# Query and key of the second mixer: one product of 512 columns in place of two of 256, and banks shared anew

## The reference

```python
def mlstm_mixer(h, w_in, b_i, b_f, g_head, w_out):
    proj = (h @ w_in).astype(jnp.float32)
    q, k, v, o, i_raw, f_raw = jnp.split(
        proj, np.cumsum([ML_QK_WIDTH, ML_QK_WIDTH, ML_V_WIDTH, ML_V_WIDTH, ML_HEADS]).tolist(), axis=-1)
    ...
    _, hs = lax.scan(_mlstm_chunk_step, init, (qc, kc, vc, ic, fc))
    ...
    out = (jax.nn.sigmoid(o) * hs).astype(h.dtype)
    return out @ w_out
```

## Time and profile before

| | |
|---|---|
| median of three runs | 1743.56 us |
| lowest, highest | 1743.27, 1744.08 us |
| the profiled execution | 1744.14 us, its span 1742.4 us |
| TensorE busy | 90% of the span |
| VectorE busy | 42% |
| ScalarE busy | 24% |
| mixer of layer 1: first group | 875.24 to 955.98 us |
| its groups 1, 2, 3 | from 955.98, 1027.38, 1098.78 to 1170.19 us |
| its output stage | 1170.19 to about 1276 us |

### The profile page before, as it was taken

The page is one execution under the profiler, slowest core; times in us unless marked ns, Lnnn a source line. Parts: engine busy times, 40 slices in busy tenths (PEclk is TensorE's granted clock), DMA queues, the critical chain, the costliest instruction groups (busy, mean ns, idle before and its releaser), DMA issues.

```text
span 1742.4 us, 25494 instructions
## 1 busy us (share of the span) xinstructions
PE 1572.3 (90%) x9954; PEld 1080.8 (62%) x9954; DVE 731.9 (42%) x1170; ACT 424.3 (24%) x572; POOL 44.4 (3%) x70
## 2 busy tenths in 40 slices
PE   8999999999997789778899999999999887688776
PEld 8999999888544244324397988988864343234322
DVE  5544444443342233222364857657434332233213
ACT  6344343433000000000154333333320000000002
POOL 0010000100100000000011000000000000000000
PEclk9999999999998998889799999999999998898888
DMA  7645455578999999999954465575799999999996
GB/s 259 212 153 177 153 169 182 209 288 308 381 423 423 426 426 424 425 427 425 412 180 159 154 195 172 165 265 206 252 368 424 426 424 424 427 426 424 425 426 243
DMA packets 160785, 543.88 MB, mean 312 GB/s; under 512 B 17504, under 2 KB 34064, under 8 KB 127824
## 3 DMA queue, kind: packets, MB, share of 16 engines
q1 hardware_dynamic: 151232, 541.12, 79.8%
q10 hardware_dynamic: 9040, 0.49, 0.3%
q0 software_dynamic: 448, 1.36, 0.2%
HBM read 540.83 MB, written 2.10 MB: 312 GB/s over the span
## 4 chain that ended last, share of the span: by engine, by line
PE 68%; DMA 21%; SPq 5%; DVE 2%; issue 1%; ACT 1%; DVEq 0%; ACTq 0%
PE psum_G L755 35%; DMA ring<-in_moe_w 21%; PE psum_S L755 18%; PE psum_A L755 9%; SPq L556 5%; PE psum_T L755 5%; DVE w_lo L434 1%; ACT w_hi L430 1%; PE psum_A L762 0%; DMA x<-in_x 0%; ACT arena L1308 0%; DVE x L1855 0%; DVE h L2108 0%; PE psum_T L1009 0%; PE psum_T L762 0%
## 5 line engine op out<-in xcount | busy, mean ns | idle before, releaser
L755 PE MATMUL psum_A<-ring,arena 128*32 128x512 f32 x1984 | 289.4, 713 | 133.5 <-DMA ring<-in_moe_w 130.8
L434 DVE TENSOR_TENSOR w_lo<-ring,w_hi 128x2048 fp32r<-128x2048 f32 x126 | 289.1, 2298 | 280.5 <-ACT w_hi L430 278.3
L430 ACT CAST w_hi<-ring 128x2048 fp32r<-128x2048 f32 x127 | 241.9, 1906 | 238.5 <-PE psum_G L755 152.2
L755 PEld LDWEIGHTS psum_A<-ring,arena 128*32 128x32 f32 x1984 | 67.2, 120 | 301.6 <-issue 300.4
L1988 DVE COPY arena_two<-psum_A 128x512 f32<-128x512 f32 x64 | 44.3, 692 | 365.7 <-PE psum_T L755 336.3
L2020 DVE TENSOR_TENSOR x<-x,psum_S 128x512 f32<-128x512 f32 x128 | 88.0, 688 | 166.8 <-PE psum_S L755 166.8
L755 PE MATMUL psum_G<-xT_hi,w_hi 128*128 128x256 f32 x512 | 149.5, 292 | 0.0
L755 PE MATMUL psum_G<-xT_hi,w_lo 128*128 128x256 f32 x512 | 145.0, 283 | 0.0
L755 PE MATMUL psum_G<-xT_lo,w_hi 128*128 128x256 f32 x512 | 145.0, 283 | 0.0
L1517 ACT ACTIVATE arena<-psum_T 128x64 f32<-128x64 f32 x64 | 14.4, 224 | 473.4 <-PE psum_T L755 473.4
L755 PE MATMUL psum_G<-arena,h 128*128 128x128 f32 x1024 | 126.8, 284 | 0.0
(11 more groups left out here) (244 smaller groups left out, 2150.6 us busy)
## 6 DMA issues: line engine op xcount, KB each, us to landing
ring<-in_moe_w SPq DMA_DIRECT2D x368, 1024.0 KB, 19.1
ring<-in_ml_w_in SPq DMA_DIRECT2D x48, 1024.0 KB, 5.1
ring<-in_sb_w_in SPq DMA_DIRECT2D x47, 1024.0 KB, 5.1
ring<-in_sb_w_out SPq DMA_DIRECT2D x16, 1024.0 KB, 5.0
turned_slots<-in_moe_w SPq DMA_DIRECT2D x16, 1024.0 KB, 13.2
ring<-in_ml_w_out SPq DMA_DIRECT2D x16, 1024.0 KB, 5.1
x<-in_x SPq DMA_DIRECT2D x4, 512.0 KB, 8.2
out_x<-h SPq DMA_DIRECT2D x4, 512.0 KB, 2.7
```

Of the source, the lines that this page charges most:

```text
L430: act.copy(w_hi[:, slot_place(j), :], ring[:, slot_place(j), :]).then_inc(hi_made, 1)
L434: dve.tensor_tensor(w_lo[:, slot_place(j), :], ring[:, slot_place(j), :], w_hi[:, slot_place(j), :].bitcast(F32), ALU.subtract).then_inc(l ...
L755: return pe.matmul(dst, lhsT, rhs, start=start, stop=stop, skip_group_check=True)
```

## The change

Query and key no longer share a bank. Query goes into `G{hd}` (slots 0, 1), key into `S{hd}` (slots 2, 3). For each block, one product moves `xT_pair[:, :, k, :]`, the high and the low part of the turned x side by side (2 x 256 columns), past the high part of the weights into the whole bank; a second one moves the high part past the low weights into the first half. The two halves of the bank must then be added when they are taken out: VectorE copies the second half into `qkT` and adds the first. For the query this is a step of its own at position 17 (`take_query`); the key is taken at the old place, and then both are multiplied with the row of scales. The head scores wait for `query_key_ready` instead of the emptied banks. Values move from S to G and the gate from G to S in layer 1; layer 0 stays as it is.

```diff
+QUERY_STEPS = [(17, "query", 0)]
...
-    SCHEDULES[_layer, "group"] = schedule(_steps, 14, GROUP_ENDS)
+    SCHEDULES[_layer, "group"] = schedule(_steps + (QUERY_STEPS if _layer else []), 14, GROUP_ENDS)
...
-        xT_hi = sb("xT_hi", [P, KT, T], F32R)
-        xT_lo = sb("xT_lo", [P, KT, T], F32R)
+        xT_pair = sb("xT_pair", [P, 2, KT, T], F32R)
+        xT_hi, xT_lo = xT_pair[:, 0], xT_pair[:, 1]
...
-        def group_bank(c, b):
-            return f"{'GSG'[c]}{b}"
+        def group_bank(layer, c, b):
+            return f"{('GSG', 'SGS')[layer][c]}{b}"
...
-                            begin(hd)
+                            bank = f"{'GS'[j // 2]}{hd}"
+                            if j % 2 == 0:
+                                claim(bank, chunk_use(1, i, 0, hd) if j else query_use(i, hd))
...
-                                last = three_turned(psum[f"G{hd}"][:, (j // 2) * T:(j // 2 + 1) * T], k,
-                                                    (slot_place(j), slice(kk * FF + hd * P, kk * FF + (hd + 1) * P)),
-                                                    k == 0, k == KT - 1)
-                                if k == KT - 1 and j == 3:
-                                    last.then_inc(filled[f"G{hd}"], 1)
+                                part = slice(kk * FF + hd * P, kk * FF + (hd + 1) * P)
+                                mm(psum[bank][:, :].rearrange("p (n t) -> p n t", n=2), w_hi[:, slot_place(j), part],
+                                   xT_pair[:, :, k, :], k == 0, False)
+                                last = mm(psum[bank][:, 0:T], w_lo[:, slot_place(j), part], xT_hi[:, k, :], False, k == KT - 1)
+                                if k == KT - 1:
+                                    last.then_inc(filled[bank], 1)
...
                     if k == 0:
-                        wait_chunk(1, g, 0)
+                        pe.wait_ge(query_key_ready, g * MLG + MLG)
...
+                elif layer and c == 0:
+                    sum_halves(1, [chunk_filled(1, i, 0, n) for n in range(MLG)], "S")
+                    for n in range(MLG):
+                        dve.tensor_tensor(qkT[:, n, :, :], qkT[:, n, :, :], rstd_row.unsqueeze(1).to_broadcast([P, 2, T]), ALU.mult)
+                    dve.drain().then_inc(query_key_ready, MLG)
...
+            def sum_halves(m, ready, banks):
+
+                for n in range(MLG):
+                    dve.wait_ge(*ready[n])
+                    dve.tensor_copy(qkT[:, n, m, :], psum[f"{banks}{n}"][:, T:2 * T])
+                dve.drain()
+                for n in range(MLG):
+                    bank = f"{banks}{n}"
+                    dve.tensor_tensor(qkT[:, n, m, :], qkT[:, n, m, :], psum[bank][:, 0:T], ALU.add).then_inc(emptied[bank], 1)
+                dve.drain()
+
+            def take_query(i):
+
+                sum_halves(0, [(filled[f"G{n}"], query_use(i, n) + 1) for n in range(MLG)], "G")
```

More of the change, by code:

```diff
@@ L114 @@
 for _layer, _steps in ((0, SB_STEPS), (1, ML_STEPS)):
-    SCHEDULES[_layer, "first"] = (schedule(GATE_STEPS, 14, GROUP_ENDS) if _layer else
+    SCHEDULES[_layer, "first"] = (schedule(GATE_STEPS + QUERY_STEPS, 14, GROUP_ENDS) if _layer else
                                   schedule(FIRST_X_STEPS, 14, FIRST_X_ENDS, split_from=3))
-    SCHEDULES[_layer, "group"] = schedule(_steps, 14, GROUP_ENDS)
+    SCHEDULES[_layer, "group"] = schedule(_steps + (QUERY_STEPS if _layer else []), 14, GROUP_ENDS)
     SCHEDULES[_layer, "out"] = schedule(_steps, 16, OUT_ENDS, 0.75, ROUTER_STEPS)
@@ L138, in bank_uses @@
             phase(("gates", layer), T=1, A=ML_HEADS // 2)
[L139 removed]
+        phase(("mix", layer), G=2 * NGROUP, S=(2 if layer else 1) * NGROUP, T=(3 if layer else 2) * NGROUP, A=(1 if layer else 2) * NGROUP)
         phase(("out", layer), G=2, S=2)
@@ L372, in turned_bank, with chunk_use, query_use @@
             return order[u], first_use["norm_mix", layer][order[u]] + order[:u].count(order[u])
-        def group_bank(c, b):
-            return f"{'GSG'[c]}{b}"
+        def group_bank(layer, c, b):
+            return f"{('GSG', 'SGS')[layer][c]}{b}"
+        def chunk_use(layer, i, c, b):
+            if layer:
+                return i * 2 + (first_use["mix", 1][group_bank(1, c, b)] + (c > 0))
+            return i * (1 if c == 1 else 2) + (first_use["mix", 0][group_bank(0, c, b)] + c // 2)
         def chunk_filled(layer, i, c, b):
-            bank = group_bank(c, b)
-            return filled[bank], i * (1 if c == 1 else 2) + (first_use["mix", layer][bank] + c // 2 + 1)
+            return filled[group_bank(layer, c, b)], chunk_use(layer, i, c, b) + 1
+        def query_use(i, hd):
+            return i * 2 + first_use["mix", 1][f"G{hd}"]
         def out_filled(layer, c, b):
@@ L392, in value_parts @@
             c = value_chunk(layer)
-            bank = group_bank(c, b)
+            bank = group_bank(layer, c, b)
             if layer:
@@ L415, in split_was_read @@
                 done = sum(1 for _, m in OUT_ORDER[:j + 1] if m < 3)
-                return split_read, layer * (9 * NGROUP + 12) + 9 * NGROUP + done
+                return split_read, layer * (9 * NGROUP + 12) + (8 if layer else 9) * NGROUP + done
             c = j // 4
@@ L419, in split_was_read @@
                 return chunk_filled(layer, i, c, 1)
+            if layer and j == 1:
+                return filled["G1"], query_use(i, 1) + 1
+            if layer:
+                return split_read, i * 8 + (9 * NGROUP + 12 + 3 * c + j % 4 + 1 - (j > 1))
             return split_read, i * 9 + (layer * (9 * NGROUP + 12) + 3 * c + j % 4 + 1)
@@ L890, in begin @@
                         if j % CSLOT == 0:
-                            bank = group_bank(c, n)
-                            claim(bank, i * (1 if c == 1 else 2) + (base[bank] + c // 2))
+                            claim(group_bank(layer, c, n), chunk_use(layer, i, c, n))
                     if layer == 0 and isinstance(i, int) and i == 0 and j == 0:
@@ L932, in project @@
                                 event(8 * j + 4 * (hd // 2) + kk)
-                            bank = group_bank(c, hd // 2)
+                            bank = group_bank(0, c, hd // 2)
                             last = three_turned(psum[bank][:, (hd % 2) * T:(hd % 2 + 1) * T], k,
@@ L944, in project @@
                                 event(8 * j + 4 * b + kk)
-                                last = three(psum[group_bank(c, b)][:, :], (xT_hi, xT_lo), b, k,
+                                last = three(psum[group_bank(layer, c, b)][:, :], (xT_hi, xT_lo), b, k,
                                              (slot_place(j), slice(kk * COLS, (kk + 1) * COLS)), k == 0, k == KT - 1)
                                 if k == KT - 1:
-                                    last.then_inc(filled[group_bank(c, b)], 1)
-                    if j % CSLOT != 3:
+                                    last.then_inc(filled[group_bank(layer, c, b)], 1)
+                    if j % CSLOT != 3 and not (layer and j == 1):
                         last.then_inc(split_read, 1)
             def wait_chunk(layer, i, c):
-                base = first_use["mix", layer]
                 for b in range(TB):
-                    bank = group_bank(c, b)
-                    pe.wait_ge(emptied[bank], i * (1 if c == 1 else 2) + (base[bank] + c // 2 + 1))
+                    pe.wait_ge(emptied[group_bank(layer, c, b)], chunk_use(layer, i, c, b) + 1)
             def sb_step(g, step, k):
@@ L1405, in ml_group @@
                         for b in range(TB):
-                            bank = group_bank(2, b)
+                            bank = group_bank(1, 2, b)
                             act.wait_ge(*chunk_filled(1, i, 2, b))
@@ L1689, in common_step @@
                         scale_router(layer)
+                if step == "query":
+                    take_query(i)
                 if step == "rstd":
```

10 lines of the change are left out of this document (5 added, 5 removed).

## The result

| | before | after |
|---|---|---|
| median | 1743.79 us of 9 (1742.25 to 1745.85) | 1747.68 us of 9 (1744.39 to 1751.05) |
| the profiled execution, its span | 1744.14, 1742.4 us | 1744.39, 1742.7 us |

What follows compares the result with a forecast made beforehand. TensorE was taken to bound the kernel. First group -0.81, three groups +3.36 and boundary -0.36 gave +2.2 us, added to the median of 1743.56 for 1745.8 us; range 1741.5 to 1748.3.

Steps and rivals of the forecast that it cites:

- The products: Second mixer's query and key products: one of 512 and one of 256 columns replace three of 256, saving 0.81 us a group.
- VectorE's addition: Copies, sums and scale products for query and key add 3.75 us of VectorE work between the splits of slots 4 and 7.
- D: VectorE time the edit adds between the splits of slots 4 and 7, predicted 3.75 us, bounds 2.7 to 4.6.
- What is late next: In three groups slot 7's low part comes late, TensorE waits, and each group becomes 1.12 us longer.
- Slot 6: Its low part of the weights comes at 1063.95 and is wanted at 1064.85, so in time.
- The turn: Ahead of slot 7, TensorE's turn waits for gated values: ready at 1068.9 against 1068.95, a tie.
- the fourth rival: VectorE's gap-free stretch gives way, the 0.45 us before 1065.58 swallowing part: +1 us, 1744.6; chance 0.68 together with the forecast.
- The first group: It has no head steps; the query frees its banks by 898.8, just in time for the values, so it keeps its 0.81 us.
- The boundary: Behind the last group a 0.82 us TensorE gap goes as bank G is free; about 0.36 us is kept.
- the first (the work hides): VectorE's added work hides if D is under 2.1 us: 3.6 us gained, 1740.0; chance 0.10.
- The second (D of 4.2 and more): VectorE's steps are dearer and the wait before slot 7 grows: at D of 4.6, +4.7 us, 1748.3; chance 0.18.
- the third: The large product's two-piece operand is slow on TensorE: up to +29 us, 1773; chance 0.03.

Runs made afterwards that it cites:

- one piece: The changed kernel with high and low part of each block side by side in memory, so the large product reads one contiguous operand: 1.0017 of the kernel before.
- the query early: The changed kernel with the query step moved from position 17 to 15, ahead of the split of slot 4: 0.9985 of the kernel before.
- the edit made alone: The kernel before with only the output stage's banks swapped, in both layers, to start on S instead of G: 1.0001 of the kernel before.

## Why the prediction was right

**The products.** A pair takes 0.347 us in steady state, 0.227 + 0.1198 as priced. The two pieces cost nothing: one piece gave the same groups. The steady group with nothing late is 70.62 to 70.63 us, 0.77 under before, for 0.81 predicted. One sum beside it is wrong: by the formula of the Trainium skill ("TensorE: Matmul & The Clock Gate", Back-to-back issue gap) a pair saves 2 x 109.2 - 215.8, about 2.5 ns and not 2.9, or 0.16 us a group. The 0.012 us that a pair saved decides against that price either way.

**VectorE's addition.** D was 3.64 us for 3.75 predicted. The query took 1.67 and not 1.77: the two drains show as gaps of 0.08 and 0.10 between its instructions and the next ones, instead of 0.13. The key took 1.97 for 1.98.

**What is late next.** Slot 7 begins 0.80 us later and restarts for 0.32, 1.12 together, as predicted. The groups are 72.50 and 72.52. Slot 6 was in time: the view of waits of after's third stretch has this one line for TensorE's products.

```profile
PE psum_G L768 <- DVE w_lo L447: 1.4, 1, 1.4
```

The turn was predicted as a tie, and came 0.1 us late, which costs nothing ahead of a wait of 1.4. The idle time ahead of join 0, which the fourth rival counted on, stayed (0.46 before 1070.69, for 0.45). In the first of the three groups, 72.82, VectorE has one more idle time, with nothing that the profile names as its releaser:

```profile
979.25 0.17 DVE L1744 TENSOR_SCALAR arena<-arena 128x2 f32<-128x2 f32 x1 [0.43 <-issue]
```

The later two have none there. The place was free of slack, and the group is 0.3 us longer than they are. The prediction left this term out.

**The first group** is the term that was mis-sized: -0.81 predicted, -0.16 measured. Of the 0.65 between them, 0.38 is the pairs at 0.353 instead of 0.347: slot 3 ended 0.43 us earlier than before (23.89 us after the start for 24.32), not 0.81. Another 0.21 comes of a misread row. The prediction took one split as 2.29 us, where the earlier trace rows have 5.31 for two at that very place, 0.83 more than the 4.48 elsewhere. VectorE in time, after:

```profile
894.90 3.10 DVE L447 TENSOR_TENSOR w_lo<-ring,w_hi 128x2048 fp32r<-128x2048 f32 x1
897.93 0.74 DVE L1691 COPY arena<-psum_G 128x256 f32<-128x256 f32 x2
```

And GpSimd at the same time:

```profile
894.78 1.08 POOL L749 TENSOR_SCALAR_AFFINE_SELECT arena<-arena 8x1024 f32<-8x1024 f32 x1
```

So the query left its banks free at 899.5 and not 898.8, and values (899.34, 1.60 for six products instead of 1.39) waited 0.2 for it. With the query early this split begins only when GpSimd's mask has ended, two splits take 4.49 again, the wait is gone (the six value products take 1.39), and the first group takes 80.30. The Trainium skill ("SBUF — State Buffer", Who interferes with whom) says that a VectorE instruction with two SBUF inputs contends with a GpSimd instruction that reads SBUF, and that the order of issue decides who blocks. The trace agrees: the split, with two such inputs, is 0.81 us longer while the mask of 1.08 us, begun 0.12 before it, runs; the query's two copies, with their input from PSUM, take 0.76 beside the same mask in the kernel with the query early, for 0.74 elsewhere.

**The boundary** gave 0.43 for 0.36 (104.75 to 104.32): the gap of 0.82 is gone, and the turn waits 0.32 for gated values. That the number fits is luck. The step as predicted, a free bank with VectorE's queue as before, gives 0.05: the turn then begins 0.39 us earlier, as priced, but its first work behind the new wait takes 0.63 for 0.44, which the prediction left out here, and most of the rest is lost by the end of the stage. The other 0.38 goes with the idle time of 0.5 on VectorE, which before has and after lacks; nothing in the prediction stood for it.

**The sum** in the profile is 402.74 - 399.70 = +3.04 for the mixer, +2.2 predicted: 0.65 of the difference is the first group, 0.27 the head groups, nearly all in the first, and -0.07 the boundary. The interval of the measured +3.3 holds both. (The time for D = 4.2 comes to 1747.1, not 1747.0.) The forecast time of 1745.8 was 1.9 us under the median measured, of which the mixer accounts for 0.85; the rest is within what the stages that the edit doesn't touch vary by. Of the rivals, the first (the work hides) is refuted in its place and confirmed in its condition: with D under 2.1 us the kernel is some 2 to 3 us faster than before (3.6 priced). The second (D of 4.2 and more) did not come, with D at 3.64, the third is refuted by the one piece, and the fourth by groups of 72.5.

## What to carry to other kernels

When TensorE is the bound and its operands are made just in time, ask between which two deadlines of the other engine's queue new work lands, and what idle time lies between them; the busy share says nothing (50.57 us of VectorE cost 1.9 us a group at one place and nothing at another). A saving on the bounding engine ahead of such a deadline is spent waiting at it, so price the late operand first, and try a move of the added work across a split before giving an edit up. And read a duration at the place where it will stand, not from the group's typical value: the row for two splits held the 0.8 us that the forecast missed. A term can also come out right for another reason than the one it was priced by, as the boundary did: only the edit made alone told the two apart.

## What the runs showed of the hardware, unexpected

- In the first group of the mixer a 512-column product with a 256-column one costs 0.353 us from about 879 us on, for 0.347 later, at the same granted clock of 1.00; the 256-column products of before took 0.120 there as elsewhere, and the 512-column ones of the values 0.227. One piece or two makes no difference; with the query early the last ten pairs of slot 3 take 3.48 us for 3.53. The cause is open.
- VectorE has single idle times of 0.43 to 0.50 us for which the profile names no releaser, at places that differ from kernel to kernel (L1744 and L1789 above). In after's first head group about 0.3 us goes with one of them, and 0.38 in "out". What they are is open.
- One profile's span can't decide 1 to 4 us in this kernel: the stretch behind the second mixer, which no experiment edits, took from 464.5 to 468.6 us over the profiles, and the expert stage of layer 0 from 454.6 to 458.6.
